# Even-block attentions: moved group ends, longer score ring, two probability-sum buffers, gating from PSUM, band mask added in PSUM

## The reference

```python
ka, va = concat([c_ak, ak]), concat([c_av, av])      # A: 256 context + 1024 latent keys
oa = softmax(qa @ ka.T * scale) @ va                 # every latent query sees all 1280 keys
# B: keys of the own block of 128 queries and of both neighbours, |distance| <= 128, plus context;
#    one sink value per head is a further column of the softmax
ob = softmax(concat([qb @ kb.T * scale + bias, sink]))[..., :-1] @ vb
y_lat = concat([oa * silu(ag), ob * silu(bg)]) @ w_out
# context queries: the same, against the 256 context keys alone
```

## Time and profile before

| | us |
|---|---|
| median of 3 runs (lowest, highest) | 3530.72 (3527.99, 3532.56) |
| the profiled execution, its own time | 3532.62 |
| span of the profiled execution | 3530.8 |
| PE busy / DVE / ACT / POOL | 3281.2 / 1340.9 / 710.4 / 380.2 |
| A: first score product to end of last multiply | 262.7 to 577.1 |
| B: first score product to end of last multiply | 760.6 to 982.2 |
| mean granted clock of PE | 0.96 of full |

### The profile page before, as it was taken

How to read it: one execution, slowest core, us unless ns; L and a number is a source line. 1 busy time by engine, 2 the same in 40 slices (tenths; PEclk the granted TensorE clock), 3 DMA queues, 4 the chain that set the end, 5 groups by cost and what they waited for, 6 DMA issues and landing times.

```text
span 3530.8 us, 27181 instructions
## 1 busy us (share of the span) xinstructions
PE 3281.2 (93%) x11342; PEld 1705.4 (48%) x11342; DVE 1340.9 (38%) x1692; ACT 710.4 (20%) x877; POOL 380.2 (11%) x244
## 2 busy tenths in 40 slices
PE   7897888987799999998999998999999999999998
PEld 4453345644455444447884533454444444444443
DVE  3727773357655169214661311034222222221001
ACT  3106551013300100014441122112001111110000
POOL 0004662004300000008220000000000000000000
PEclk9999998998899999999999999999999999999998
DMA  6000001010042101014110101000101111110011
GB/s 231 24 30 1 1 1 36 25 55 1 1 155 90 32 17 54 30 34 112 26 35 30 31 12 48 30 18 24 36 30 36 42 36 42 36 46 33 33 49 48
DMA packets 38042, 145.61 MB, mean 41 GB/s; under 512 B 4928, under 2 KB 5440, under 8 KB 35872
## 3 DMA queue, kind: packets, MB, share of 16 engines
q1 hardware_dynamic: 31680, 126.40, 10.6%
q0 software_dynamic: 6240, 17.47, 2.1%
HBM read 139.66 MB, written 6.82 MB: 41 GB/s over the span
## 4 chain that ended last, share of the span: by engine, by line
PE 85%; DVE 6%; issue 3%; ACT 3%; POOL 2%; DMA 1%; SPq 0%; DVEq 0%; ACTq 0%; POOLq 0%
PE ps L677 49%; PE ps L1151 9%; PE ps L1091 4%; PE ps L1044 3%; PE ps L810 3%; PE ps L838 3%; PE ps L973 2%; POOL x_ctx L602 2%; DVE x_ctx L1732 1%; PE ps L825 1%; PE ps L903 1%; PE ps L932 1%; PE ps L921 1%; PE ps L1068 1%; PE ps L785 1%
## 5 line engine op out<-in xcount | busy, mean ns | idle before, releaser
L677 PE MATMUL ps<-arena 128*128 128x512 f32 (+1 forms) x4192 | 1716.2, 571 | 22.8 <-ACT arena L1203 7.6
L677 PEld LDWEIGHTS ps<-arena 128*128 128x128 f32 x4192 | 799.4, 191 | 930.9 <-issue 904.6
L1151 PE MATMUL ps<-arena 128*128 128x512 f32 x704 | 302.3, 592 | 0.0
L1920 DVE SCALAR_TENSOR_TENSOR arena<-ps,vectors,arena 128x1023 f32<-128x1023 f32 x44 | 56.4, 1283 | 461.5 <-ACT arena L1416 461.5
L1151 PEld LDWEIGHTS ps<-arena 128*128 128x128 f32 x704 | 133.8, 190 | 168.4 <-issue 168.4
L903 PE MATMUL ps<-arena 64*128 64x512 f32 x504 | 156.7, 704 | 31.2 <-DVE x_ctx L1732 26.9
L1416 ACT ACTIVATE arena<-ps,vectors 128x1024 f32<-128x1024 f32 x44 | 52.9, 1203 | 537.5 <-PE ps L677 537.5
L1822 DVE SCALAR_TENSOR_TENSOR x_ctx<-arena,vectors,x_ctx 128x1024 f32<-128x1024 f32 x120 | 154.2, 1285 | 4.3
L1783 DVE TENSOR_TENSOR x_lat<-ps,x_lat 128x1024 f32<-128x1024 f32 x16 | 19.6, 1224 | 354.6 <-PE ps L1151 281.8
L1091 PE MATMUL ps<-arena 128*128 128x512 f32 x256 | 131.3, 637 | 11.7 <-ACT arena L1401 11.7
L810 PE MATMUL ps<-arena,x_ctx 128*128 128x512 f32 (+2 forms) x384 | 132.7, 430 | 8.9 <-ACT arena L1262 7.2
(11 more groups left out here) (214 smaller groups left out, 2986.5 us busy)
## 6 DMA issues: line engine op xcount, KB each, us to landing
arena<-in_wall SPq DMA_DIRECT2D x188, 512.0 KB, 3.6
arena<-expanded_bias POOLq DMA_DIRECT2D x80, 160.0 KB, 3.9
arena<-in_wdown SPq DMA_DIRECT2D x8, 1408.0 KB, 6.1
x_lat<-in_xl_in SPq DMA_DIRECT2D x4, 1024.0 KB, 9.5
x_lat<-in_xl_in SPq DMA_DIRECT2D x2, 2048.0 KB, 9.7
out<-x_lat SPq DMA_DIRECT2D x8, 512.0 KB, 3.1
expanded_bias<-in_rpb POOLq DMA_DIRECT2D x1, 2560.0 KB, 17.8
x_ctx<-in_dmask POOLq DMA_DIRECT2D x5, 320.0 KB, 3.5
```

What stands on the lines that cost most here:

```text
L677: mm = pe.matmul(ps[:, o + c:o + c + n], W[:, ring_of(g) % WSLOTS, k, :], rhs(k, c, n), start=(k == 0), stop=(k == KT - 1))
L1151: mm = pe.matmul(ps[:, o + c:o + c + n], WD[m % 2][:, k, :], ACTV[:, k, c:c + n], start=(k == 0), stop=(k == DOWN_K - 1))
```

## The change

The plan: B starts one step later (`first[g+1]+2+j`), M1 is moved to the step after M0, and OE, DEN and MIX come three, four and five steps after the last B. PV stays two steps after B. OE is no longer ACT's copy but a DVE multiply of the gates by PV_O straight from PSUM; MIX's multiply follows in its own step, and O_EVAC is gone. The mask is added in place in PSUM by DVE, and ACT fills every item. In DVE's queue the mask comes first; in the step of NB the maximum comes before the subtraction, else after it; then reductions, OE, reciprocal, multiply. The ring has 18 slots in A (five of them in the gate rows 4 to 7, which B writes later) and 13 in B, and its area's last slot is the second sum buffer. x is loaded again only after B, in four pairs of tiles, each before the late weights of its tile, and four evO weights are loaded before B ends.

```diff
@@ group_plan
-        at = max(at + 1, first[g + 1] - 1 + 2)
+        at = max(at + 1, first[g + 1] + 2)
...
-            steps[first[g + 1]]["MT"] = g
+            steps[first[g + 1]]["M0"] = g
+            steps[first[g + 1] + 1]["M1"] = g
             steps[at]["NB"] = g
         if j == sizes[g] - 1:
             steps[at + 3]["OE"] = g
-            steps[at + 3]["DEN"] = g
-            steps[at + 4]["MIX"] = g
+            steps[at + 4]["DEN"] = g
+            steps[at + 5]["MIX"] = g
@@ rings
-        RING_A = [XL[:, k, :] for k in range(KT)] + [area(SCR + 1024 * i, 1024) for i in range(6)]
-        RING_B = [XL[:, k, :] for k in range(4, KT)] + [area(SCR + 1024 * i, 1024) for i in range(5)]
+        LOW = [XL[:, k, :] for k in range(KT)] + [area(SCR + 1024 * i, 1024) for i in range(6)]
+        HIGH = [area(22016 + 4 * TOK + 1024 * i, 1024) for i in range(5)]
...          # A: LOW + HIGH, B: LOW;  "ring": ring[:-1], "sums": [PROB_SUM, ring[-1]]
@@ POOL
+                    total = at["sums"][g % 2]
                     if j == 1:
-                        if g:
-                            pool.wait_ge(at["den"], g)
+                        if g >= 2:
+                            pool.wait_ge(at["den"], g - 1)
@@ PE, in a step: NB, F, then
-                    if "MT" in st:
-                        max_transposes(st["MT"], 0)
+                    for half in range(2):
+                        if f"M{half}" in st:
+                            max_transposes(st[f"M{half}"], half)
                     if "PV" in st:
...
-                    if "MT" in st:
-                        max_transposes(st["MT"], 1)
@@ ACT
-                    if "OE" in st:
...
-                        act.activation(O_EVAC, ps[:, PV_O:PV_O + BANK], ACT.Copy).then_inc(at["o_out"], 1)
-                    if "F" in st and not at["is_masked"][st["F"]]:
+                    if "F" in st:
                         n = st["F"]
-                        act.wait_ge(at["st"], n + 1)
+                        if at["is_masked"][n]:
+                            act.wait_ge(at["masked"], sum(at["is_masked"][:n + 1]))
+                        else:
+                            act.wait_ge(at["st"], n + 1)
@@ DVE, in a step
+                    if "F" in st and at["is_masked"][st["F"]]:
...
+                        dve.tensor_tensor(s, s, groups[g]["keys"][j][1].unsqueeze(1).to_broadcast([P, HEADS, P]), ALU.add)\
+                           .then_inc(at["masked"], 1)
+                    if "NB" in st and "F" in st:
+                        maximum(st["F"])
+                    if "B" in st:
+                        subtract(st["B"])
+                    if "F" in st and "NB" not in st:
+                        maximum(st["F"])
...          # reductions of M0 or M1
+                    if "OE" in st:
+                        g = st["OE"]
+                        gv = mixed_in(g)
+                        dve.wait_ge(at["pv"], first[g + 1])
+                        dve.tensor_tensor(gv, ps[:, PV_O:PV_O + BANK].rearrange("p (m q) -> p m q", m=4), gv, ALU.mult)\
+                           .then_inc(at["o_out"], 1)
...          # DEN: reciprocal; MIX: the multiply from MISC, after o_out, then_inc(at["mixed"], 1)
@@ SP
-                if g == GBASE["evB"] + WSLOTS:
-                    sp.wait_ge(soft["A"]["mixed"], 10)
-                    sp.dma_start(XL[:, 0:4, :], xl_in[:, 0:4, :]).then_inc(x_back[0], 16)
...
+                    for m in range(WSLOTS):
+                        load_weight(g + 4 * m)
                     sp.wait_ge(soft["B"]["mixed"], 10)
+                    for m in range(KT):
+                        if m < KT // 2:
+                            sp.dma_start(XCv[:, 2 * m:2 * m + 2, :], xc_in[:, 2 * m:2 * m + 2, :]).then_inc(x_back[m], 16)
+                            sp.dma_start(XL[:, 2 * m:2 * m + 2, :], xl_in[:, 2 * m:2 * m + 2, :]).then_inc(x_back[m], 16)
+                        for i in range(3 * m, 3 * m + 3):
...          # the three late weights of tile m, from m = 1 on after late_t
```

More of the change, by code:

```diff
@@ L272, in program @@
         rows_in_sbuf = sem("modulation_rows_in_sbuf")
[L273 removed]
+        x_back = [sem(f"residual_pair{i}_back") for i in range(KT // 2)]
         q_padded = sem("queries_padded")
@@ L415, in in_ring @@
         def in_ring(at, n):
-            k = sum(at["is_masked"][:n + 1])
-            return (at["masked"], k) if at["is_masked"][n] else (at["filled"], n + 1 - k)
+            return at["filled"], n + 1
         def scores_read(at, n):
@@ L600, in prob_sums @@
                         pool.wait_ge(at["pooled"], pooled_upto(at, n) - 1)
-                        one = PROB_SUM
-                    pool.tensor_tensor(PROB_SUM, one, ring[n % len(ring)], ALU.add).then_inc(at["pooled"], 1)
+                        one = total
+                    pool.tensor_tensor(total, one, ring[n % len(ring)], ALU.add).then_inc(at["pooled"], 1)
             prob_sums(soft["A"])
@@ L1698, in soft_attention, with mixed_in @@
                 ring, groups, items, first = at["ring"], at["groups"], at["items"], at["first"]
-                for st in at["plan"]:
[L1700 to L1705, removed]
-                        dve.tensor_tensor(p, ps[:, NM_BC:NM_BC + 1024], p, ALU.add).then_inc(at["shifted"], 1)
-                    if "F" in st:
+                def mixed_in(g):
+                    c0, c1 = groups[g]["q"]
+                    return G[:, at["g_rows"]:at["g_rows"] + 4, c0:c1]
@@ new lines, in subtract, with maximum @@
+                def subtract(n):
+                    g, j = items[n]
+                    if j == 0:
+                        dve.wait_ge(at["bcast"], g + 1)
+                    p = ring[n % len(ring)]
+                    dve.tensor_tensor(p, ps[:, NM_BC:NM_BC + 1024], p, ALU.add).then_inc(at["shifted"], 1)
+                def maximum(n):
+                    g, j = items[n]
+                    if j == 0:
+                        return
+                    o = S_T + 2 * (n % 2) * BANK
+                    dve.wait_ge(*in_ring(at, n))
+                    if j == 1:
+                        dve.wait_ge(*in_ring(at, n - 1))
+                        if g:
+                            dve.wait_ge(at["max_t"], 2 * g)
+                        one = ring[(n - 1) % len(ring)]
+                    else:
+                        dve.wait_ge(at["maxed"], at["max_before"][g] + j - 1)
+                        one = KEY_MAX
+                    dve.tensor_tensor(KEY_MAX, ps[:, o:o + 2 * BANK], one, ALU.max).then_inc(at["maxed"], 1)
@@ new lines, in soft_attention @@
+                    for half in range(2):
+                        if f"M{half}" not in st:
+                            continue
+                        g = st[f"M{half}"]
+                        nm = ST[:, g % 4, 1, :]
+                        dve.wait_ge(at["max_t"], 2 * g + half + 1)
+                        dve.tensor_reduce(nm[:, 4 * half:4 * half + 4],
+                                          ps[:, MISC:MISC + BANK].rearrange("p (h k) -> p h k", h=4), AX_X, ALU.max,
+                                          negate=True).then_inc(at["reduced"], 1)
+                        if half == 0:
+                            continue
```

83 lines of the change are left out of this document (21 added, 62 removed).

## The result

The changed kernel takes 3586.02 us (median of 4 runs, 3584.15 to 3594.24) against 3531.64 (3527.99 to 3533.09) for the one before, measured beside it: ratio 1.016, 95% interval 1.0142 to 1.0178. It is 54 us slower; the forecast was 33.

What follows compares the result with a forecast made beforehand. It took both attention stages to be bound by a chain of waits between engines, no engine being full. A +14, B +18.6 and loads 0 gave +33 us, a median of 3564 us, range 3528 to 3588.

Steps and rivals of the forecast that it cites:

- A, six cycles: Steady groups of attention A: period 36.2 us against 33.5, +2.7 each, six times, +16 us.
- B, four cycles: Steady groups of attention B: period 28.3 us against 25.3, four times, +12 us.
- The clock term of A: Steady groups of A: PE work slowed by the lower clock after PV0's wait, 2.5 us per group, bounds 0 and 4.
- The tail of B: After B's last NB: no wait for PROB_SUM, twelve steps as before, -3 us.
- The second short cycle of B: Second of the two short cycles after B's first NB: +2 us.
- The walked 25.35: Steady group of B: time from one NB to the next in the walked chain, before the clock's +3 us.
- the late weights: Loads after B's end: first late weights come about 3.4 us later behind an x pair, hidden from PE by 0.7; 0 us.
- The mask add writing PSUM: Masked tiles in B: DVE's mask add into PSUM takes 1.21 us, as the add into the ring did.
- Rival (c): POOL still holds the ring slots, so old stalls stay beside the new one: +1.6 us per group, 3585 us; chance 0.05.
- Rival (d): The late weights miss PE and the low clock holds to the end of each MIX: 3595 us; chance 0.07.
- Rival (b): The order wait before PV0 is there, but the clock falls no further: A -1, B +4, 3534 us; chance 0.16.
- Rival (a): A and B: removed waits decide, DVE reaches OE soon after the last PV; 3480 us; chance 0.12.

Runs made afterwards that it cites:

- filler6: The changed kernel with six unused 128x512 products on PE ahead of PV0 of the groups: 3562.6 us, ratio 1.0079 to the kernel before.
- sink_psum: The changed kernel with the sink minimum's constant first copied to PSUM in seven of B's ten groups, sink addition after NB's signal: 3577.6 us.
- oe_first: The changed kernel with the multiply by O moved to the front of its step on DVE's queue: 3532.8 us, ratio 1.0007 to the kernel before.
- both: The changed kernel with the multiply by O first in its step and the subtraction ahead of the maximum in NB's step: 3495.0 us, ratio 0.9899.
- ring_only: The kernel before with only the longer rings, two sum buffers and later loads of x: 3507.7 us, ratio 0.9932 to the kernel before.

## Why the prediction fell short

Direction, mechanism and the main waits were right, three fifths of the size were there, and the time lay just inside the range. The steps of the sum, profiled execution against profiled execution:

| step | forecast | measured |
|---|---|---|
| A, NB of the first group | +1.7 | +1.7 |
| A, first cycle | +2.5 | +1.5 |
| A, six cycles | +16 | +20.7 |
| A, tail | -6 | -5.2 |
| B, first NB | +3 | +4.3 |
| B, two short cycles | +2.3, +2 | +2.2, +8.5 |
| B, four cycles | +12 | +14.3 |
| B, the one before the tail | +2.3 | +4.3 |
| B, tail | -3 | +6.1 |
| loads | 0 | within 1 |

The forecast adds up to 33 and the profiled executions to 61.6. Of the 28.6 between them 21.0 lie in B, above all in its tail (9.1) and its second short cycle (6.5), 4.4 in A and 3.2 ahead of A.

**The clock term of A, "I take 2.5 lost per group", was mis-sized.** Against the 33.5 that filler6 takes at full clock, the six cycles of A lose 1.5, 4.4, 4.2, 4.2, 4.1 and 2.4, on average 3.5. In the group shown first the rows say how: from PV0 on, PV 0.90 too long, F 0.95, PV 0.65, a later PV 0.78, MIX 0.89, 4.2 in all. DEN (1.95) and the F behind it (1.13), in their midst, ran at full clock. The cycle of 35.0 has the same wait, and only two long rows behind it:

```profile
331.27 1.98 PE L921 MATMUL ps<-arena 128*64 128x256 f32 x8 [5.58 <-DVE arena L1756]
333.18 1.65 PE L902 MATMUL ps<-arena 64*128 64x512 f32 x4
```

I had halved the clock over a part of the 8 us from PV0 to F7 that I didn't name; which part it is differs from cycle to cycle. It differs between executions too: in sink_psum, where A is the same program, the six cycles lose 2.9 on average and are 17 us longer than before, against 16 forecast. So 2.5 was too low in both, by 0.4 and by 1.0 a cycle.

**The tail of B, "-3 (no wait for PROB_SUM; twelve steps as before)", failed.** Only the wait that goes was counted. I never walked the queue of DVE and PE for a step in which M0, PV0, OE and DEN meet. PE in that tail:

```profile
996.55 1.09 PE L878 MATMUL ps<-consts,x_ctx 128*128 128x128 f32 x4 [2.60 <-DVE softmax_stats L1742]
...
1002.46 2.93 PE L921 MATMUL ps<-arena 128*64 128x256 f32 x16 [2.16 <-DVE arena L1756]
1005.31 3.58 PE L930 MATMUL ps<-consts,x_ctx 128*128 128x2 f32 x16
...
1019.07 1.08 PE L921 MATMUL ps<-arena 128*64 128x256 f32 x8 [2.01 <-DVE arena L1756]
...
1021.48 3.58 PE L930 MATMUL ps<-consts,arena 128*128 128x2 f32 x16
```

A wait for a reduction, two of over 2 us for the multiply by O, and a lower clock (0.69 for 0.79): the first two DENs take 3.58 each, where the first two of before take 1.92 and 1.95. With the multiply first (oe_first) the same tail takes 38.8, 8 less than before, at a clock of 0.87. The wait of 2.60 is there too, those for the multiply are down to one of 1.15. So the multiply's place, not the plan, cost it.

**The second short cycle of B, "+2", failed in the same way.** A group of four tiles has its OE in that step too:

```profile
830.23 1.98 PE L921 MATMUL ps<-x_lat,arena 128*64 128x256 f32 x8 [3.95 <-DVE arena L1756]
832.13 3.58 PE L930 MATMUL ps<-consts,x_ctx 128*128 128x2 f32 x16
...
847.74 1.09 PE L889 MATMUL ps<-consts,softmax_stats 128*128 128x128 f32 x8 [3.13 <-DVEq L1751]
```

Here 3.95, a DEN at half speed, and 3.13 before NB, half of it the sink's minimum (1.49). I had said that PV0 and OE share a step for every group size, and priced it in the long groups alone.

**What was missing: the sink operation.** It explains the extra of B's steady groups and part of the second short cycle: some 1.25 a group ahead of NB, and 13.2 less in B with it cured (8.4 between medians). The walked 25.35 with these 1.25 is 26.6, which filler6 takes in a cycle at a clock of 0.94. The four cycles of after take 28.9 on average, so the low clock cost about 2.3 there, less than the 3 that I took. The prediction cites the Trainium skill (SBUF — State Buffer, Who interferes with whom) for the two multiplies; the same rule names this operation, which I passed over because its row was short. The trace agrees with the rule in both, 0.68 against 2.52 for the multiply and 0.17 against 1.09 to 1.42 for the sink's operations.

**Right for the given reason:** the late weights. Their first row, and PE's product that needs the result; they answer to the earlier trace rows:

```profile
1053.33 0.87 DVE L1564 TENSOR_SCALAR arena<-arena,silu_c 128x384 f32<-128x384 f32 x2 [10.35 <-DMA arena<-in_wall]
```

```profile
1062.60 1.40 PE L761 MATMUL ps<-consts,arena 128*128 128x2 f32 x12
```

The wait is 10.35 for 6.91, +3.4 as worked out, and PE came to its late product 19.6 after B's end against 19.3: hidden. The mask add writing PSUM takes 1.23 on average (1.21 taken). Rival (c) fell with POOL's two releases of 0.6. Rival (d) fell in its first half with the late weights. Its second half, a low clock to the end of each MIX, came nearer than my term in four of A's six cycles: MIX takes 1.93 there for 1.04, though with full clock in between. Rival (b) fell with the granted clock of A's cycles, 0.86 in four, 0.90 and 0.95 in two, where before had 0.90 to 1.00. Rival (a) named its point of decision rightly: whether OE starts before the maximum of F4. It does in oe_first and both, not in after; with both orders mended the time is 3495, where (a) had 3480.

What stays open: what decides how many rows behind the same wait run at the low clock, and where the mask is better written. I did not separate the part of the low clock in B from the queue there beyond filler6, whose products also delay the groups with shorter waits.

## What to carry to other kernels

Where an engine waits for a result, ask what stands ahead of that result's operation on its own queue, and walk the short groups and the tail too, not only the steady group: moving one 0.68 us multiply to the front of DVE's step was worth 53 us. A gap on PE is to be priced with what runs behind it at 1.2 GHz instead of 2.4; here 5.6 of waiting cost 1.5 to 4.4 more. And a shift of a schedule changes which short DVE operations meet GpSimd, so each one with both inputs in SBUF ahead of a signal needs a look.

## What the hardware showed that I had not expected

- An operation of 128x8 on DVE with both inputs in SBUF took 0.17 when GpSimd was idle and 1.42 beside one of its adds, ending 0.03 after the add did; with one input in PSUM it took 0.17. The price is the rest of the other engine's instruction, not a share of the operation's own length.
- The time lost behind a wait isn't in proportion to it, nor always the same for the same wait. Behind 5.58 and behind 3.31 the first PV took 1.98 and 1.97, behind 1.19 it took 1.08. But behind the same 5.58 two, three or five PE rows were long, and the cycle took 35.0, 35.9 or 37.7.
- The low clock also came without a long wait. With longest waits before PE of 1.3 and 1.4, three of the six cycles of A in ring_only and four in both show a granted clock of 1.00, and the others 0.90 to 0.95. In both, a cycle with the usual 1.19 and 1.44 has an F of 1.76 and a PV of 1.97.
